# Opening of a mixed mLSTM/S5 decoder step: x turned before the sample state's rows, its squares summed on TensorE, the second weight slab split later

## The chip, the cores and the metric

One Trainium2 chip, one core. The metric is the device time of one execution in microseconds (us), the median of several runs.

## What is computed

One inference step of a two-layer trunk on 576 tokens of 1024 channels: 512 of a fresh prompt and 64 of eight sample sequences (8 tokens each). Layer 0 is an mLSTM matrix memory with 8 heads, layer 1 a grouped complex-diagonal S5 state space; each layer is followed by a squared-ReLU MLP with 4096 hidden channels. What the change touches is the very first norm and the first product:

```
def rms_norm(x, g):
    y = xf * lax.rsqrt(jnp.mean(xf * xf, axis=-1, keepdims=True) + EPS)
    return (y * g)
def mlstm_mixer(x, w_in, ...):
    proj = jnp.einsum('bld,de->ble', x, w_in)      # 1024 -> 3088 columns
    q, k, v, o, gi, gf = jnp.split(proj, ...)
```

All data are float32.

## The kernel before, in words

The activations lie turned: `x[:, k]` holds channels 128k to 128k+127 on the partitions and the 576 tokens along the free axis, so x is 8 tiles (k = 0 to 7; KT = 8) of 128x576. Weights come in slabs of 1024x128 (8 blocks of 128x128), 145 of them. Each slab is used in two parts that together keep float32 precision: ScalarE writes the rounded part `whi` (`split_hi`, L363), VectorE the rest `wlo` (`split_lo`, L368). The activations are split the same way: `prep_hi` (ScalarE, L431) writes `xg_hi`, the rounded x times gain, and `prep_lo` (VectorE, L436) the rest, `xg_lo`. A `product` (L384) is, for each of the 8 tiles, 3 combinations (hi·hi, lo·hi, hi·lo) for 2 halves of 288 tokens: 48 matmuls, shown as 24 pairs. The norm's factor 1/rms is not applied to the input but to the product: `R` holds it for all tokens, and `scale_in` (L1334) multiplies while it takes a slab's result out of PSUM. So product 0 can run before the factor is known, but its result can't leave PSUM.

The order of the work is written out by hand, one program for each engine, tied by semaphores. Each engine executes strictly in its program's order. The opening:

- **SyncE** issues the loads of x (L479, L481), slabs 0 and 1 (L356), the eight rows of the sample state `st_n` (L486, into `nrow`), some small vectors, the S5 matrix `craw`, then slabs 2 and 3. Slab 2 waits for `w_ready` 1 (slab 0 split), slab 3 for `w_ready` 2.
- **TensorE** turns the gains `vrow` (L1847), then the state's rows `nrow` (L1849, waiting for `nrow_in`), then x (loop at L1850 to L1857): for each tile k four 128x128 transposes and one for the 64 sample tokens, into PSUM banks 0/1 or 2/3 in turn. Tile k waits until VectorE has taken out tile k-2. Then product 0, the sum of squares over partitions (`stats`, L394: ones times `acc`, into banks 4 and 5), product 1, product 2, the gate rows (L1873).
- **VectorE** copies the gains and then `nT` (L1318) out of PSUM, then for each tile copies x out (L1324, L1325) and writes `xg_lo` of the tile before; `split_lo` of slab 0 stands after tile 3, that of slab 1 at the end. Then the reciprocal (`inv_rms`, L405), `scale_in` of slab 0, `split_lo` of slab 2, and so on in turn.
- **ScalarE** splits slabs 0 and 1, then for each tile `prep_hi` and the square of x (tile 0 into `acc`, L958; the others alternately into `sqb` and `qkvo[:, 23]`, L962, waiting from k = 3 on until the buffer is free). Then the square root (`rms`, L400).
- **GpSimd** (`square_sums`, L459) adds the squares of tiles 1 to 7 to `acc`, one 128x576 addition a tile.

The same `square_sums` serves the later norms (stages 1 to 3), where it both squares and adds; these stages stay as they are, with their semaphore counts moved.

Of the kernel before, what the change touches and what calls it, by code (L numbers as in the profile page):

```python
# [83 lines left out]
def build(nc, x_prompt, x_sample, st_C, st_n, st_m, st_re, st_im, g_mix, g_ffn, g_fin, w_in, b_i, b_f,  # L84
# [16 lines left out]
    with ctx:  # L101
# [337 lines left out]
        sq0 = (sqb[:], qkvo[:, 23])  # L439

        ACC0 = (0, 8, 16, 23, 31, 36)

        def square_sums(pool, stage):

            n0 = ACC0[stage]
            if stage:
                wait_x(pool, stage, 0)
                nc.gpsimd.tensor_tensor(acc[:], x[:, 0], x[:, 0], ALU.mult).then_inc(acc_done, 1)
            for k in range(1, ACC0[stage + 1] - n0):
                pool.wait_ge(acc_done, n0 + k)  # L450
                if stage:
                    wait_x(pool, stage, k)
                    nc.gpsimd.tensor_tensor(sqb[:], x[:, k], x[:, k], ALU.mult).then_inc(sq_done, 1)
                    pool.wait_ge(sq_done, n0 - KT - (stage - 1) + k)
                    sq = sqb[:]
                else:
                    pool.wait_ge(sq0_done, k)
                    sq = sq0[k % 2]
                nc.gpsimd.tensor_tensor(acc[:], acc[:], sq, ALU.add).then_inc(acc_done, 1)  # L459
# [17 lines left out]
        def _(sp):  # L477
# [26 lines left out]
            def load_u_row(h):  # L504
                if h < 2:
                    sp.wait_ge(ub_out, 16)
                    sp.wait_ge(acc_done, ACC0[1])
                else:
                    sp.wait_ge(exp_done, h - 1)
                sp.dma_start(Ub[h % 2], d_ub[h:h + 1, :].to_broadcast([P, L])).then_inc(ub_in[h % 2], 16)  # L510
# [191 lines left out]
        def _(pool):  # L702
# [9 lines left out]
            square_sums(pool, 0)  # L712
# [214 lines left out]
            pool.wait_ge(sq0_done, 9)  # L927
            nc.gpsimd.tensor_tensor(acc[:], squares[:, 0], squares[:, 1], ALU.add).then_inc(acc_done, 1)  # L928
            for k in range(2, 6):
                pool.wait_ge(sq0_done, 8 + k)  # L930
                pool.wait_ge(acc_done, ACC0[4] + k - 1)
                nc.gpsimd.tensor_tensor(acc[:], acc[:], squares[:, k % 4], ALU.add).then_inc(acc_done, 1)

        @block.scalar
        def _(act):
# [17 lines left out]
            split_hi(act, 1, 0)  # L953
            act.wait_ge(vec_ready, 1)
            for k in range(KT):
                prep_hi(act, k, 0, 0, 0, V_MIX0)
                if k == 0:
                    nc.scalar.activation(acc[:], x[:, 0], ACT.Square).then_inc(acc_done, 1)  # L958
                else:
                    if k >= 3:  # L960
                        act.wait_ge(acc_done, k - 1)
                    nc.scalar.activation(sq0[k % 2], x[:, k], ACT.Square).then_inc(sq0_done, 1)  # L962
# [331 lines left out]
        def _(dve):  # L1294
# [22 lines left out]
            dve.wait_ge(vec_pe, 2)  # L1317
            V.tensor_copy(nT[:], ps[:, 7, 0:32]).then_inc(vec_ready, 1)  # L1318

            for k in range(KT + 1):  # L1320
# [7 lines left out]
                if k in (3, KT):  # L1328
                    split_lo(dve, 0 if k == 3 else 1, 0)
            def scale_in(base, j, t):  # L1330
# [513 lines left out]
        def _(pe):  # L1844
# [3 lines left out]
            pe.wait_ge(nrow_in, 16 * 8)  # L1848
            nc.tensor.transpose(ps[:, 7, 0:32], nrow[:], ident[0:32, 0:32]).then_inc(vec_pe, 1)  # L1849
            pe.wait_ge(x_in, 16 * 5)  # L1850
            for k in range(KT):
# [397 lines left out]
            for a in (acc, tbuf, R):  # L2249
                if a is tbuf:  # L2250
                    pe.wait_ge(sq0_done, 14)
                elif a is R:
                    pe.wait_ge(sq7_done, 2)
# [37 lines left out]
```

## Time and profile before

| | |
|---|---|
| median of 3 runs | 1352.79 us (1350.94 to 1354.02) |
| the profiled execution | 1348.39 us |
| its span in the trace | 1346.6 us |
| TensorE busy | 1295.8 us (96%) |
| VectorE, ScalarE, GpSimd busy | 791.3, 490.5, 355.4 us |
| TensorE's weight loads busy | 1258.2 us (93%) |
| HBM traffic | 121 MB, 90 GB/s over the span |

The span is what the trace covers, from the first instruction to the last; the execution's own time is 1.8 us longer. TensorE is the engine that is nearly always busy, so what counts is where it is idle, where it runs at its lower clock, and how much work it is given. Times within the trace are counted from the span's start.

### The profile page before, as it was taken

What the parts mean: (1) busy time and instruction counts of PE and PEld (TensorE: products, weight loads), DVE (VectorE), ACT (ScalarE), POOL (GpSimd) and SP (SyncE); (2) the same over time, 40 slices, a digit from 0 to 9 for tenths busy, and PEclk for the clock granted to TensorE, in tenths of its full rate; (3) what the DMA queues carried; (4) which work ended last, traced back from release to release, by engine and by line L of the source; (5) the groups of instructions that cost most, each with busy time, mean ns of one, the idle gap of its engine ahead of it and who ended that gap; (6) DMA issues with size and microseconds to landing.
All of it is one profiled execution on the core that took longest, in us unless ns stands there. A gap on an engine that the chain in (4) does not pass through costs nothing.

```text
span 1346.6 us, 24669 instructions
## 1 busy us (share of the span) xinstructions
PE 1295.8 (96%) x9953; PEld 1258.2 (93%) x9953; DVE 791.3 (59%) x1118; ACT 490.5 (36%) x743; POOL 355.4 (26%) x360
## 2 busy tenths in 40 slices
PE   4999999999999999999999899999999999999997
PEld 2999998789999999999999888999999999999997
DVE  5673336867764673342354666343687586686785
ACT  4321136532431331331341124422552442543553
POOL 3001005535899970000027661112000000000001
PEclk9999999999999999999999777999999999999999
DMA  5223332324232232223225995224223323223222
GB/s 150 64 79 85 86 94 73 89 54 104 76 94 79 78 89 82 78 84 87 78 74 150 145 141 125 81 79 124 72 70 94 94 71 116 65 94 96 83 72 71
DMA packets 223039, 121.81 MB, mean 90 GB/s; under 512 B 34752, under 2 KB 218744, under 8 KB 222976
## 3 DMA queue, kind: packets, MB, share of 16 engines
q1 hardware_dynamic: 222144, 120.74, 35.1%
q8 instruction: 42, 0.69, 0.2%
q10 hardware_dynamic: 832, 0.21, 0.1%
q14 instruction: 21, 0.17, 0.1%
HBM read 110.18 MB, written 10.75 MB: 90 GB/s over the span
## 4 chain that ended last, share of the span: by engine, by line
PE 81%; DVE 9%; SPq 3%; DMA 2%; ACT 2%; issue 2%; POOL 1%; ACTq 0%; DVEq 0%; POOLq 0%
PE ps L384 63%; PE ps L2175 12%; DVE wlo L368 1%; PE ps L2131 1%; SPq L628 1%; PE ps L2127 1%; DMA late<-d_taps 1%; SPq L647 1%; DMA Cst<-in_state_mlstm_C 1%; DMA out<-Cst 1%; DVE R L405 1%; DVE x L1660 1%; PE ps L1942 0%; DVE xg_lo L436 0%; DVE hid_lo L1583 0%
## 5 line engine op out<-in xcount | busy, mean ns | idle before, releaser
L384 PE MATMUL ps<-xg_hi,whi 128*128 128x288 f32 x1424 | 304.9, 295 | 3.2 <-DVE wlo L368 1.7
L384 PE MATMUL ps<-xg_hi,wlo 128*128 128x288 f32 x1424 | 304.4, 295 | 0.0
L384 PE MATMUL ps<-xg_lo,whi 128*128 128x288 f32 x1424 | 303.7, 294 | 0.0
L363 ACT ACTIVATE whi<-raw 128x1024 fp32r<-128x1024 f32 x115 | 121.5, 1058 | 353.6 <-PE ps L384 334.1
L384 PEld LDWEIGHTS ps<-xg_hi,whi 128*128 128x128 f32 x1424 | 228.2, 188 | 5.5 <-issue 2.3
L384 PEld LDWEIGHTS ps<-xg_hi,wlo 128*128 128x128 f32 x1424 | 227.7, 188 | 0.0
L384 PEld LDWEIGHTS ps<-xg_lo,whi 128*128 128x128 f32 x1424 | 227.6, 188 | 0.0
L368 DVE TENSOR_TENSOR wlo<-raw,whi 128x1024 fp32r<-128x1024 f32 x115 | 170.3, 1481 | 76.3 <-ACT whi L363 76.2
L384 PE MATMUL ps<-hid_hi,whi 128*128 128x288 f32 x896 | 192.6, 296 | 2.5 <-DVE hid_lo L1805 2.2
L384 PE MATMUL ps<-hid_lo,whi 128*128 128x288 f32 x896 | 192.1, 295 | 0.0
L384 PE MATMUL ps<-hid_hi,wlo 128*128 128x288 f32 x896 | 190.9, 294 | 0.0
L384 PEld LDWEIGHTS ps<-hid_hi,whi 128*128 128x128 f32 x896 | 143.3, 188 | 4.1 <-DVE hid_lo L1805 2.9
L384 PEld LDWEIGHTS ps<-hid_hi,wlo 128*128 128x128 f32 x896 | 143.8, 188 | 0.0
L384 PEld LDWEIGHTS ps<-hid_lo,whi 128*128 128x128 f32 x896 | 143.6, 188 | 0.0
L1561 DVE TENSOR_TENSOR x<-x,ps 128x576 f32 (+1 forms) x40 | 30.2, 754 | 124.7 <-PE ps L384 124.7
L928 POOL TENSOR_TENSOR acc<-hB 128x576 f32<-128x576 f32 x1 | 1.8, 1767 | 350.9 <-ACT hB L1163 350.9
L2175 PE MATMUL ps<-hB_hi,whi 128*128 128x288 f32 x256 | 76.0, 297 | 0.6 <-DVE x L1660 0.6
L1579 DVE TENSOR_TENSOR tbuf<-rbuf,R 128x576 f32<-128x576 f32 x32 | 35.6, 1112 | 68.2 <-ACT rbuf L1067 68.1
L2175 PE MATMUL ps<-hB_hi,wlo 128*128 128x288 f32 x256 | 75.5, 295 | 0.0
L2175 PE MATMUL ps<-hB_lo,whi 128*128 128x288 f32 x256 | 75.4, 294 | 0.0
L1660 DVE TENSOR_TENSOR x<-x,ps 128x288 f32<-128x288 f32 x112 | 50.4, 452 | 32.4 <-PE ps L2175 32.0
L1334 DVE TENSOR_TENSOR qkvo<-ps,R 128x576 f32 (+1 forms) x25 | 18.9, 756 | 77.4 <-PE ps L384 77.3
(401 smaller groups left out, 2066.9 us busy)
## 6 DMA issues: line engine op xcount, KB each, us to landing
raw<-in_ffn_w_up SPq DMA_DIRECT2D x64, 512.0 KB, 4.0
raw<-in_ffn_w_down SPq DMA_DIRECT2D x32, 512.0 KB, 4.2
raw<-in_ffn_w_down SPq DMA_DIRECT2D x16, 1024.0 KB, 5.2
raw<-in_mlstm_w_in SPq DMA_DIRECT2D x25, 512.0 KB, 3.7
raw<-in_s_w_glu SPq DMA_DIRECT2D x16, 512.0 KB, 3.9
raw<-in_mlstm_w_out SPq DMA_DIRECT2D x8, 512.0 KB, 4.2
late<-d_taps SPq DMA_DIRECT2D x32, 128.0 KB, 7.6
d_u<-unat SPq DMA_DIRECT2D x8, 288.0 KB, 2.8
```

The lines of the kernel that those rows point to most:

```text
L363: nc.scalar.activation(whi[:, s], raw[:, s], ACT.Copy).then_inc(whi_done, 1)
L368: nc.vector.tensor_tensor(wlo[:, s], raw[:, s], whi[:, s].bitcast(F32), ALU.subtract).then_inc(w_ready, 1)
L384: last = nc.tensor.matmul(ps[:, 2 * s + c, 0:HN], w[:, s, k, :], a[:, k, c * HN:(c + 1) * HN], start=(k == 0 and n == 0), stop=(k == KT - ...
L405: nc.vector.reciprocal(R[:], R[:]).then_inc(R_ready, 1)
L628: sp.dma_start(U2[i * GC:(i + 1) * GC, g, :], d_u.rearrange("(g c) t b -> t c g b", c=GC)[T - 1 - i, :, g]).then_inc(u2_in[half], 16)
L647: sp.dma_start(taps_pair[j][i * GC:(i + 1) * GC], d_taps[2 * j * P:(2 * j + 2) * P, i * GC:i * GC + P].rearrange("(g c) m -> c g m", c=GC) ...
L1334: V.tensor_tensor(halves(tile(qkvo, t)), slab_ps(s), halves(R[:]), ALU.mult).then_inc(ps_free[s], 1)
L1561: V.tensor_tensor(halves(tile(x, m)), halves(tile(x, m)), slab_ps(s), ALU.add).then_inc(ps_free[s], 1)
L1579: V.tensor_tensor(tbuf[:], rbuf[:], R[:], ALU.mult).then_inc(scaled, 1)
L1660: V.tensor_tensor(xh, xh, ps[:, bank, 0:HN], op).then_inc(x_added, 1)
L2127: nc.tensor.matmul(o[g2], taps_of[k][:, 2 * q + g2, :], U2[:, 8 * k + 2 * q + g2, :], start=True, stop=False)
L2175: last = nc.tensor.matmul(out, w[wi][:, k, :], hi[:, k, t, :], start=(first and k == 0 and n == 0), stop=(k == 3 and n == 2), skip_group_c ...
```

## The change

- TensorE's program turns x right after the gains; the turn of `nrow` stands behind the eight tiles of x, and VectorE's copy `nT` behind its split of slab 1.
- ScalarE writes the squares of all 8 tiles into 8 buffers of their own (`qkvo[:, 16]` to `qkvo[:, 23]`, which slabs fill only later), without waiting for anyone.
- GpSimd has no part in stage 0. `squares_sum(k)` on TensorE multiplies the squares of tile k by ones and accumulates over the tiles in PSUM banks 4 and 5: two float32 matmuls of 288 columns for each tile. Tiles 0 to 5 stand between the transposes of x (behind tile k+2), tiles 6 and 7 inside product 0, before its last two tiles. The old `stats` for stage 0 goes.
- `split_hi` of slab 1 stands behind ScalarE's tile 3, not before tile 0.
- The loads of the first two u rows no longer wait for `acc`.

```diff
-        sq0 = (sqb[:], qkvo[:, 23])
-
-        ACC0 = (0, 8, 16, 23, 31, 36)
+        sq0 = [qkvo[:, 16 + k] for k in range(KT)]
+
+        ACC0 = (0, 0, 8, 15, 23, 28)
...
                 if h < 2:
                     sp.wait_ge(ub_out, 16)
-                    sp.wait_ge(acc_done, ACC0[1])
...
             nc.gpsimd.memset(gw[:, AM, 0:TS + 1:T], 0.0).then_inc(am_ready, 1)
-            square_sums(pool, 0)
...
             split_hi(act, 0, 0)
-            split_hi(act, 1, 0)
             act.wait_ge(vec_ready, 1)
             for k in range(KT):
                 prep_hi(act, k, 0, 0, 0, V_MIX0)
-                if k == 0:
-                    nc.scalar.activation(acc[:], x[:, 0], ACT.Square).then_inc(acc_done, 1)
-                else:
-                    if k >= 3:
-                        act.wait_ge(acc_done, k - 1)
-                    nc.scalar.activation(sq0[k % 2], x[:, k], ACT.Square).then_inc(sq0_done, 1)
+                nc.scalar.activation(sq0[k], x[:, k], ACT.Square).then_inc(sq0_done, 1)
+                if k == 3:
+                    split_hi(act, 1, 0)
             rms(act, 0)
...
             V.tensor_copy(vec[:].rearrange("p v k -> p (v k)"), ps[:, 4, 0:56]).then_inc(vec_ready, 1)
-            dve.wait_ge(vec_pe, 2)
-            V.tensor_copy(nT[:], ps[:, 7, 0:32]).then_inc(vec_ready, 1)
-
             for k in range(KT + 1):
...
                     split_lo(dve, 0 if k == 3 else 1, 0)
+            dve.wait_ge(vec_pe, 2)
+            V.tensor_copy(nT[:], ps[:, 7, 0:32]).then_inc(vec_ready, 1)
...
-            pe.wait_ge(nrow_in, 16 * 8)
-            nc.tensor.transpose(ps[:, 7, 0:32], nrow[:], ident[0:32, 0:32]).then_inc(vec_pe, 1)
             pe.wait_ge(x_in, 16 * 5)
+
+            def squares_sum(k):
+                if k == 0:
+                    pe.wait_ge(vec_ready, 1)
+                    pe.wait_ge(const_done, 2)
+                pe.wait_ge(sq0_done, k + 1)
+                for c in range(2):
+                    last = nc.tensor.matmul(ps[:, 4 + c, 0:HN], ones[:], sq0[k][:, c * HN:(c + 1) * HN],
+                                            start=(k == 0), stop=(k == KT - 1))
+                if k == KT - 1:
+                    last.then_inc(stat_done, 1)
+
             for k in range(KT):
...
                 nc.tensor.transpose(ps[:, r + 1, 0:TS], xtok[0:TS, 0, k * P:(k + 1) * P],
                                     ident[0:TS, 0:TS]).then_inc(xt_done, 1)
+                if k >= 2:
+                    squares_sum(k - 2)
+            pe.wait_ge(nrow_in, 16 * 8)
+            nc.tensor.transpose(ps[:, 7, 0:32], nrow[:], ident[0:32, 0:32]).then_inc(vec_pe, 1)
             pe.wait_ge(x_ready, KT - 1)
-            pe.wait_ge(const_done, 2)
             xg, hid = (xg_hi, xg_lo), (hid_hi, hid_lo)
-            product(pe, 0, 0, xg, (xg_ready, 0))
-            pe.wait_ge(vec_ready, 1)
-            stats(pe, 0)
+            product(pe, 0, 0, xg, (xg_ready, 0), range(KT - 2))
+            for k in range(KT - 2, KT):
+                squares_sum(k)
+            product(pe, 0, 0, xg, (xg_ready, 0), range(KT - 2, KT))
             pe.wait_ge(x_ready, KT)
             product(pe, 1, 0, xg)
```

The rest of the diff moves the semaphore counts of the later stages.

TensorE's program at the start, before (`xtok` is x as loaded, `vrow` the gains, `nrow` the state's rows):

```order
L1847 MATMUL ps<-ident,vrow 128x56 [waits vec_in,const_done]
L1849 MATMUL ps<-ident,nrow 128x32 [waits nrow_in]
L1856 MATMUL ps<-ident,xtok 128x128 [waits x_in]
L1856 MATMUL ps<-ident,xtok 128x128 x3
L1857 MATMUL ps<-ident,xtok 128x64
```

and now (`ones` with `qkvo` is a square's sum; the tiles that follow repeat the last five rows):

```order
L1834 MATMUL ps<-ident,vrow 128x56 [waits vec_in,const_done]
L1853 MATMUL ps<-ident,xtok 128x128 [waits x_in]
L1853 MATMUL ps<-ident,xtok 128x128 x3
L1854 MATMUL ps<-ident,xtok 128x64
L1853 MATMUL ps<-ident,xtok 128x128 x4
L1854 MATMUL ps<-ident,xtok 128x64
L1853 MATMUL ps<-ident,xtok 128x128 [waits x_ready]
L1853 MATMUL ps<-ident,xtok 128x128 x3
L1854 MATMUL ps<-ident,xtok 128x64
L1843 MATMUL ps<-qkvo,ones 128x288 [waits sq0_done,const_done,vec_ready]
L1843 MATMUL ps<-qkvo,ones 128x288
```

The turn of x has moved ahead of that of `nrow`, and from the third tile on a sum of squares, which waits for ScalarE, stands between the tiles.

TensorE's program around the end of product 0, one piece of the difference:

```order
 L384 MATMUL ps<-xg_hi,wlo 128x288 x2
+L1843 MATMUL ps<-qkvo,ones 128x288 [waits sq0_done]
+L1843 MATMUL ps<-qkvo,ones 128x288
+L1843 MATMUL ps<-qkvo,ones 128x288 [waits sq0_done]
+L1843 MATMUL ps<-qkvo,ones 128x288
 L384 MATMUL ps<-xg_hi,whi 128x288 [waits xg_ready]
 L384 MATMUL ps<-xg_hi,whi 128x288
...
 L384 MATMUL ps<-xg_hi,wlo 128x288 x2
-L394 MATMUL ps<-acc,ones 128x288 [waits acc_done,vec_ready]
-L394 MATMUL ps<-acc,ones 128x288
 L384 MATMUL ps<-xg_hi,whi 128x288 [waits w_ready,x_ready]
```

The last two sums stand two tiles ahead of the end of product 0, where the single one stood behind it.

## Rows read from the trace of the kernel before

**Rows 1.** The page: busy time by engine.
```profile
PE 1295.8 (96%) x9953; PEld 1258.2 (93%) x9953; DVE 791.3 (59%) x1118; ACT 490.5 (36%) x743; POOL 355.4 (26%) x360
```

**Rows 2.** Chain of waits, 0 to 90 us: start, duration, what.
```profile
12.93 2.86 DMA nrow<-in_state_mlstm_n
...
39.17 0.98 PE ps L394 x4
```

**Rows 3.** Last load of x: issue, and its time to landing.
```profile
L481 SPq DMA_DIRECT2D xtok<-in_x_prompt x1: 436/436/436, 3.0 to 3.0; - x1
...
DMA to landing us min/median/max: 8.0/8.0/8.0
```

**Rows 4.** Timeline of TensorE, 16 to 35 us: start, duration, instruction, idle before.
```profile
16.08 1.11 PE L1856 MATMUL ps<-ident,xtok 128*128 128x128 f32 x4
...
17.42 1.11 PE L1856 MATMUL ps<-ident,xtok 128*128 128x128 f32 x4
...
26.88 1.12 PE L1856 MATMUL ps<-ident,xtok 128*128 128x128 f32 x4 [2.69 <-DVE x L1325]
...
33.25 0.68 PE L384 MATMUL ps<-xg_lo,whi 128*128 128x288 f32 x2
33.73 0.68 PE L384 MATMUL ps<-xg_hi,wlo 128*128 128x288 f32 x2
```

**Rows 5.** Timeline of TensorE, end of product 1 and start of product 2.
```profile
45.54 0.43 PE L384 MATMUL ps<-xg_hi,whi 128*128 128x288 f32 x2
45.80 0.42 PE L384 MATMUL ps<-xg_lo,whi 128*128 128x288 f32 x2
46.07 0.43 PE L384 MATMUL ps<-xg_hi,wlo 128*128 128x288 f32 x2
46.69 0.54 PE L384 MATMUL ps<-xg_hi,whi 128*128 128x288 f32 x2 [0.20 <-DVE wlo L368]
```

**Rows 6.** Timeline of ScalarE, 12 to 20 us.
```profile
12.88 1.06 ACT L363 ACTIVATE whi<-raw 128x1024 fp32r<-128x1024 f32 x1 [2.51 <-DMA raw<-in_mlstm_w_in]
...
18.44 0.78 ACT L431 ACTIVATE xg_hi<-x,vec 128x576 fp32r<-128x576 f32 x1 [3.05 <-DVE x L1325]
...
19.72 0.78 ACT L431 ACTIVATE xg_hi<-x,vec 128x576 fp32r<-128x576 f32 x1
```

**Rows 7.** Timeline of VectorE, 18 to 46 us.
```profile
20.33 0.69 DVE L1324 COPY x<-ps 128x512 f32<-128x512 f32 x1
...
21.78 0.69 DVE L1324 COPY x<-ps 128x512 f32<-128x512 f32 x1
...
23.68 2.41 DVE L368 TENSOR_TENSOR wlo<-raw,whi 128x1024 fp32r<-128x1024 f32 x1
...
40.96 3.75 DVE L405 RECIPROCAL R<-R 128x576 f32<-128x576 f32 x1 [3.25 <-ACT R L400]
44.74 0.76 DVE L1334 TENSOR_TENSOR qkvo<-ps,R 128x576 f32<-128x576 f32 x1
45.42 1.22 DVE L368 TENSOR_TENSOR wlo<-raw,whi 128x1024 fp32r<-128x1024 f32 x1
```

**Rows 8.** Eight transposes of the S5 matrix, later, on TensorE.
```profile
83.06 1.09 PE L1883 MATMUL ps<-ident,craw 128*128 128x128 f32 x8
```

**Rows 9.** Timeline of TensorE in the S5 layer, 775 to 841 us.
```profile
775.75 2.24 PE L2112 MATMUL ps<-U,GT 128*64 128x72 f32 x32
...
836.10 0.85 PE L384 MATMUL ps<-hid_hi,whi 128*128 128x288 f32 x2
...
840.00 0.42 PE L384 MATMUL ps<-hid_hi,wlo 128*128 128x288 f32 x2
```

**Rows 10.** Table by stretch: busy us of PE, PEld, DVE, ACT, POOL; granted clock; DMA.
```profile
770.00:775.00 5.00, 5.00 (x31) 4.34 (x30) 3.77 (x7) 0.00 (x0) 3.75 (x4) 0.50 1.39 108
775.00:780.00 5.00, 5.00 (x60) 4.65 (x58) 1.93 (x5) 2.00 (x5) 0.62 (x1) 0.66 1.29 114
...
835.00:840.00 5.00, 5.00 (x26) 4.83 (x26) 0.00 (x0) 1.88 (x4) 0.00 (x0) 0.52 0.57 128
```

More of the change, by code:

```diff
@@ L437, in prep_lo @@
                                            ALU.mult, ALU.subtract).then_inc(xg_ready, 1)
-        sq0 = (sqb[:], qkvo[:, 23])
-        ACC0 = (0, 8, 16, 23, 31, 36)
+        sq0 = [qkvo[:, 16 + k] for k in range(KT)]
+        ACC0 = (0, 0, 8, 15, 23, 28)
         def square_sums(pool, stage):
             n0 = ACC0[stage]
-            if stage:
-                wait_x(pool, stage, 0)
-                nc.gpsimd.tensor_tensor(acc[:], x[:, 0], x[:, 0], ALU.mult).then_inc(acc_done, 1)
+            wait_x(pool, stage, 0)
+            nc.gpsimd.tensor_tensor(acc[:], x[:, 0], x[:, 0], ALU.mult).then_inc(acc_done, 1)
             for k in range(1, ACC0[stage + 1] - n0):
                 pool.wait_ge(acc_done, n0 + k)
[L451 to L455, printed above, removed]
-                else:
-                    pool.wait_ge(sq0_done, k)
-                    sq = sq0[k % 2]
-                nc.gpsimd.tensor_tensor(acc[:], acc[:], sq, ALU.add).then_inc(acc_done, 1)
+                wait_x(pool, stage, k)
+                nc.gpsimd.tensor_tensor(sqb[:], x[:, k], x[:, k], ALU.mult).then_inc(sq_done, 1)
+                pool.wait_ge(sq_done, n0 - (stage - 1) + k)
+                nc.gpsimd.tensor_tensor(acc[:], acc[:], sqb[:], ALU.add).then_inc(acc_done, 1)
         def last_squares(dve, stage):
@@ L926, in _ @@
             squares = hB[:].rearrange("p (s h) c -> p s (h c)", h=2)
-            pool.wait_ge(sq0_done, 9)
+            pool.wait_ge(sq0_done, KT + 2)
             nc.gpsimd.tensor_tensor(acc[:], squares[:, 0], squares[:, 1], ALU.add).then_inc(acc_done, 1)
             for k in range(2, 6):
-                pool.wait_ge(sq0_done, 8 + k)
+                pool.wait_ge(sq0_done, KT + 1 + k)
                 pool.wait_ge(acc_done, ACC0[4] + k - 1)
@@ L956, in _ @@
                 prep_hi(act, k, 0, 0, 0, V_MIX0)
-                if k == 0:
-                    nc.scalar.activation(acc[:], x[:, 0], ACT.Square).then_inc(acc_done, 1)
-                else:
-                    if k >= 3:
-                        act.wait_ge(acc_done, k - 1)
-                    nc.scalar.activation(sq0[k % 2], x[:, k], ACT.Square).then_inc(sq0_done, 1)
+                nc.scalar.activation(sq0[k], x[:, k], ACT.Square).then_inc(sq0_done, 1)
+                if k == 3:
+                    split_hi(act, 1, 0)
             rms(act, 0)
@@ L2250, in _ @@
                 if a is tbuf:
-                    pe.wait_ge(sq0_done, 14)
+                    pe.wait_ge(sq0_done, KT + 7)
                 elif a is R:
```

## The prediction, made before the changed kernel had run

> **What bounds the kernel now.** I read the page first: TensorE is busy 96% of the span [rows 1], so the kernel gets faster only where TensorE starts earlier, waits less, has less to do or runs at a better clock. The change touches the first 40 us alone, so I then read the chain of waits and the timelines there. The reader is to see one long detour. The last part of x was issued at 3.0 and needed 8.0 us: x is there at 11.0 [rows 3]. But TensorE's next instruction is the turn of the state's rows, whose last load was issued at 12.9 and took 2.9 us [rows 2]; it ran at 15.8, and x's first transposes at 16.1 [rows 4]. Five microseconds go by with x on the chip. After that TensorE turns x, a tile every 1.34 us (16.08 to 17.42 [rows 4]), stands still for 2.7 us at 24.2 to 26.9 for VectorE (the split of slab 0 took 2.41 us [rows 7], twice the 1.22 that the same instruction on slab 2 takes once GpSimd no longer adds squares), reaches product 0 at 31.2, and is solid from there: the sum of squares runs for 0.98 us from 39.0 (39.17 in the chain, which starts it at its second matmul's record [rows 2]), product 1 follows, and product 2 begins at 46.69, some 0.35 us late, since the chain square root, reciprocal (3.75 us), scale-out of slab 0, split of slab 2 has only just ended [rows 5, 7]. The mark by which I measure is that start of product 2 at 46.69: from there on both kernels have the same program, and each engine is released by TensorE's products.
>
> **TensorE's two speeds.** A pair of 288-column matmuls starts every 0.48 us in the first three microseconds of product 0 (33.25 to 33.73 [rows 4]) and every 0.265 us later (45.54 to 46.07 in two steps [rows 5]). The same 0.48 stands in the S5 layer where the granted clock reads 0.50, and it becomes 0.26 where that goes back to 1.00 [rows 9, 10]. So the first stretch ran at the 1.2 GHz level, though no granted clock is recorded for it, and it rose to 2.4 GHz at 34.2. What the engine did before a rise: 3.0 us of product 0; 3.7 us of products (836.1 to 839.8 [rows 9]); 2.6 us of closely packed 72-column matmuls (775.75 to about 778.4, by the 0.66 of that row [rows 9, 10]). The 8 us of transposes from 16.1 on brought no rise.
>
> **The change, part by part.**
>
> *The turn of nrow moves behind x.* The gains were taken out at 10.5 already, so x starts when it is there, at 11.05 instead of 16.08: 5.0 us earlier. The nrow turn costs 0.3 us in its new place, where its load is long there. VectorE's copy of 0.2 us stands behind its split of slab 1 and nobody needs it before the gate rows.
>
> *ScalarE.* It splits slab 0 at 12.88, when the slab lands, until 13.94 [rows 6]. This is not moved and is now on the path: tile 0 of x is out of PSUM by 13.3. Rounding and squaring one tile take 1.28 us (18.44 to 19.72 [rows 6]), so the first squares are ready at about 15.3. The split of slab 1, 1.06 us, moves behind tile 3. ScalarE's eight tiles and that split take at most 8 x 1.46 + 1.06 = 12.7 us from 13.9 on (1.46 is VectorE's pace), so 27, plus a table load of 1.3: no sum has to wait for it (the last one is due above 31, below).
>
> *GpSimd's seven additions go.* They were not on TensorE's path by themselves, but VectorE was slow beside them. Without them I take VectorE's undisturbed pace, 1.45 us for a tile (20.33 to 21.78 [rows 7]) and 1.14 to 1.22 for a split. From the first copy at 12.5 that is 12.5 + 8 x 1.45 + 2 x 1.2 = 26.5, with its waits for TensorE below some 28 to 29; product 0 needs its tiles one by one from 27 on. The 2.7 us stall goes; what is late next is TensorE itself.
>
> *The squares' sum on TensorE.* One pair of float32 matmuls of 288 columns costs 0.98 us at the high clock [rows 2]; eight instead of one add 6.9 us. At the low clock the trace has none: between 0.98 x 0.48/0.265 = 1.78 and 0.98 x 2 = 1.96; I take 1.94, near the upper end, as the pair is four records of pure streaming. So from 15.3, when the first sum is released, TensorE never runs dry. All at the high clock it would have to do: 5 tiles of transposes at 0.68 (8 transposes take 1.09 [rows 8], so five 0.68) = 3.4; 8 sums x 0.98 = 7.84; nrow 0.2; product 0, 24 pairs x 0.265 = 6.36. Together 17.8, so product 1 at 33.1. Of the time c spent at the low clock half is lost. The squares are dense float32 work, so I expect the rise among them, but they are broken up by transposes: between 2.6 us (the quickest rise above) and 7 us after 15.3. I take c = 4.5, near the rises seen (3.0, 3.7) plus an allowance for the transposes between. That costs 2.25: product 1 at 35.4, its end 6.35 later at 41.7.
>
> *The square root's chain.* The last sum ends two product tiles (1.6 us) before product 1, at 33.8; square root 0.74, reciprocal 3.75, scale-out 0.76, split 1.22 [rows 7] end at 40.4, 1.3 us before 41.7. The 0.35 us wait of product 2 goes too.
>
> *Sum.* Product 2 starts at 41.7 instead of 46.7: **5.0 us saved**; with c from 2.6 to 7, 5.9 to 3.7. The later stages are released by products and shift as a whole. The loads of u rows waited on `acc` in name only, and the renumbered semaphores cost nothing. Against the profiled execution that gives 1348.4 - 5.0 = 1343.4. That execution was 4.4 us quicker than the median of the runs, 1352.8, which is what the forecast is for: **1347.8 us**. The runs lie within 3 us of each other, and about 0.2% (2.7 us) is what can be told from no change.
>
> **A rule against it.** Eight microseconds of transposes, a tile every 1.34 us, brought no rise of the clock [rows 4]. The Trainium skill (TensorE: Matmul & The Clock Gate, Part 4: PE-mode transpose) says the full clock doesn't engage for transposes, since they don't count as busy in the same way; the trace agrees, as far as those 8 us go. If that keeps the mixture low as well, the sum is that of the first rival.
>
> **The rivals.**
>
> *A, the low clock lasts through the squares (slower).* If transposes between the sums keep TensorE at 1.2 GHz, it has from 15.3 to do 6 x 1.94 + 5 x 1.34 + 0.3 = 18.6 us before product 0, which then starts at 33.9, later than the 31.2 of before. It is followed by 6.36 + 2 x 0.98 and half of another 3.0: product 1 at 43.8, product 2 at 50.2, 3.5 us later than now: 1356.3. For it: 8 us of transposes gave no rise, and they would be 40% of the mixture's time. Against it: 2.6 us of dense short matmuls behind a thinner mixture sufficed in the S5 layer. The point at which it decides: with c above about 14 us nothing is gained. Chance 0.10.
>
> *B, a late rise or a wait that takes over (no change).* With c of 10 to 14 us, or an engine that I take as covered (ScalarE's tiles behind the slab split at 13.9, VectorE, a later landing of x or slab 0) costing 3 us, the gain is 0 to 2.5: about 1351.5. For it: ScalarE and TensorE now hand each tile to one another through VectorE, with margins of a microsecond. Chance 0.18.
>
> *C, the gain arrives and is bigger.* If the rise comes within 2.6 us and transposes at the high clock are cheaper than 0.68 a tile, 6 to 6.5 us: 1346.5. It is the low side of the forecast, not a case apart.
>
> **How the numbers follow.** Forecast with C 0.72, B 0.18, A 0.10. The forecast's own range is 1345.3 (6.5 saved, and one for the runs' spread) to 1350. To hold 8 in 10 the range takes in most of B: 1345.0 to 1352.4; A and the last of each side stay out. Faster by over 0.2%: 0.72; within: 0.18; slower: 0.10.
>
> **What would show it.** Right: the first transposes of x at about 11.1, the first sum at 15.3, no gap on TensorE of more than a few tenths until product 2; a pair of sums falling from 1.9 to 0.98 us between 18 and 22; VectorE's split of slab 0 at 1.2 us; product 0 from about 27, product 2 at 41.7; later stages of the same lengths. Wrong: sums still at 1.9 us when product 0 starts (A), or TensorE idle between tiles (B), or a stage behind 50 us that has grown by what was saved.

## The result, and the profile after

The changed kernel took 1342.16 us (median of 7 runs, 1337.76 to 1344.28), the kernel before 1350.00 us (median of 7, 1345.13 to 1354.02; three of the seven are the runs that the prediction knew, the other four, 1345.13 to 1350.00, have a median of 1346.7). The ratio is 0.9948, 95% interval 0.9923 to 0.9973: 7.0 us faster, 3.6 to 10.4. (Here and below the ratio with its interval is an estimate over the runs and not the quotient of the two medians, which lie 7.8 us apart.) The predicted saving of 5.0 us lies in that interval; the predicted time of 1347.8 us is 5.6 us too high, and the measured time is outside the range. The profiled execution of the changed kernel took 1343.77 us, that of before 1348.39: 4.6 us.

The page of the changed kernel: busy time, the chain by line.

```profile
PE 1300.7 (97%) x9981; PEld 1262.1 (94%) x9981; DVE 786.0 (59%) x1118; ACT 490.2 (37%) x743; POOL 343.4 (26%) x353
...
PE ps L384 64%; PE ps L2176 12%; PE ps L2132 1%; PE ps L2128 1%; DVE wlo L368 1%; PE ps L1843 1%; DMA Cst<-in_state_mlstm_C 1%; DMA xtok<-in_x_prompt 1%; DMA late<-d_taps 1%; DMA out<-Cst 1%; DVE x L1647 1%; PE ps L1853 0%; PE ps L2113 0%; ACT qkvo L1008 0%; PE ps L2070 0%
```

Beside [rows 1]: TensorE has 28 matmul records and 4.9 us of busy time more, GpSimd 12 us less, and the span is 4.8 us shorter. An engine that is given more work finishes earlier; the time came out of its idle stretches (50.8 us before, 41.1 now). The load of x (`xtok`) has entered the chain in the place of `nrow`'s [rows 2].

TensorE's timeline of the changed kernel, 10 to 43 us (start, duration, instruction, idle before it and its releaser):

```profile
10.93 1.12 PE L1853 MATMUL ps<-ident,xtok 128*128 128x128 f32 x4 [1.55 <-DMA xtok<-in_x_prompt]
...
12.28 1.11 PE L1853 MATMUL ps<-ident,xtok 128*128 128x128 f32 x4
...
15.16 2.26 PE L1843 MATMUL ps<-qkvo,ones 128*128 128x288 f32 x4
17.21 1.06 PE L1853 MATMUL ps<-ident,xtok 128*128 128x128 f32 x4
...
18.50 1.68 PE L1843 MATMUL ps<-qkvo,ones 128*128 128x288 f32 x4
20.01 0.60 PE L1853 MATMUL ps<-ident,xtok 128*128 128x128 f32 x4
...
20.74 1.24 PE L1843 MATMUL ps<-qkvo,ones 128*128 128x288 f32 x4
21.82 0.60 PE L1853 MATMUL ps<-ident,xtok 128*128 128x128 f32 x4
...
27.33 0.24 PE L1859 MATMUL ps<-ident,nrow 32*128 32x32 f32 x1
27.50 0.53 PE L384 MATMUL ps<-xg_hi,whi 128*128 128x288 f32 x2
...
32.37 2.10 PE L1843 MATMUL ps<-qkvo,ones 128*128 128x288 f32 x8
34.09 0.65 PE L384 MATMUL ps<-xg_hi,whi 128*128 128x288 f32 x2
...
42.23 0.43 PE L384 MATMUL ps<-xg_hi,whi 128*128 128x288 f32 x2
```

Read the starts. x is turned at 10.93 (16.08 before [rows 4]), a tile every 1.35 us, the low level of the clock. The first sum takes from 15.16 to 17.21, 2.05 us; the second from 18.50 to 20.01, 1.51 us; the third from 20.74 to 21.82, 1.08 us: the clock rose to its 2.4 GHz level at about 19.4, within the second. From there on a tile and its sum take 1.81 us. No idle time stands beside any row after the first. Product 0 starts at 27.50; 42.23 is product 2's start, for there are 24 pairs before it from 35.89 on, and no wait stands there (46.69, with a wait, before [rows 5]).

VectorE's and ScalarE's timelines of the changed kernel, the rows that answer to [rows 6, 7]:

```profile
18.60 0.69 DVE L1309 COPY x<-ps 128x512 f32<-128x512 f32 x1 [1.85 <-PE ps L1854]
...
20.07 1.22 DVE L368 TENSOR_TENSOR wlo<-raw,whi 128x1024 fp32r<-128x1024 f32 x1
...
35.28 3.75 DVE L405 RECIPROCAL R<-R 128x576 f32<-128x576 f32 x1 [5.29 <-ACT R L400]
39.07 0.76 DVE L1321 TENSOR_TENSOR qkvo<-ps,R 128x576 f32<-128x576 f32 x1
39.74 1.22 DVE L368 TENSOR_TENSOR wlo<-raw,whi 128x1024 fp32r<-128x1024 f32 x1
```

```profile
12.72 1.06 ACT L363 ACTIVATE whi<-raw 128x1024 fp32r<-128x1024 f32 x1 [2.22 <-DMA raw<-in_mlstm_w_in]
13.68 0.76 ACT L431 ACTIVATE xg_hi<-x,vec 128x576 fp32r<-128x576 f32 x1
14.35 0.67 ACT L948 ACTIVATE qkvo<-x 128x576 f32<-128x576 f32 x1
...
34.51 0.74 ACT L400 ACTIVATE R<-ps,eps 128x576 f32<-128x576 f32 x1 [4.72 <-PE ps L1843]
```

The split of slab 0 takes VectorE 1.22 us, not 2.41 [rows 7]. VectorE waits for TensorE now (1.85 us), where TensorE waited 2.69 us for VectorE [rows 4]. ScalarE's first square ends at about 15.0 and releases the first sum. The chain of square root, reciprocal, scale-out and split ends at 41.0, 1.3 us before product 2 asks for its slab.

### The profile page after: what moved, and what is told of

It reads as the page before. It is cut to its first block, busy times and chain, and to the rows that moved or that the text cites. A ratio compares the mean times of both kernels' runs of the same rounds, so it can differ in the third digit from the quotient of the medians.

```text
span 1341.8 us, 24708 instructions
## 1 busy us (share of the span) xinstructions
PE 1300.7 (97%) x9981; PEld 1262.1 (94%) x9981; DVE 786.0 (59%) x1118; ACT 490.2 (37%) x743; POOL 343.4 (26%) x353
## 4 chain that ended last, share of the span: by engine, by line
PE 84%; DVE 7%; ACT 3%; DMA 2%; issue 2%; SPq 1%; POOL 1%; ACTq 0%; DVEq 0%; POOLq 0%
PE ps L384 64%; PE ps L2176 12%; PE ps L2132 1%; PE ps L2128 1%; DVE wlo L368 1%; PE ps L1843 1%; DMA Cst<-in_state_mlstm_C 1%; DMA xtok<-in_x_prompt 1%; DMA late<-d_taps 1%; DMA out<-Cst 1%; DVE x L1647 1%; PE ps L1853 0%; PE ps L2113 0%; ACT qkvo L1008 0%; PE ps L2070 0%
```

## The experiments

Times of all runs are medians of the runs beside their own runs of the kernel before. Three more readings are used below. *The gate rows' start*: where TensorE begins L1873 (53.23 in the profile before, 48.67 in that of the changed kernel, so 4.56 us earlier); it closes the part that the change touches. *The marks*: the start of the same matmul, counted back from the program's last, in two profiles. *At equal clock*: each timed run records the mean granted clock of its span; over all single runs of all kernels one line was fitted, with a level for each kernel (two for the change, one for each set of its runs). It says 1.1 us for 0.001 of mean clock, with 1.8 us of scatter about it. No granted clock is recorded before the first rise, so the opening's low stretch isn't in that mean, and the difference of two levels is what the opening is worth, as long as no recorded fall lies in it, no wait comes up later, and the change doesn't itself lower the mean clock. Where it does that, this reading leaves out a loss that the kernel has. The +/- is a 95% interval.

**The kernel before, again, twice.** Is the opening stable, and what varies?

> The kernel before itself, for a second profile of it. Theory S: its opening is the same to within a microsecond wherever it is run (the turn of nrow at 15 to 16, the gate rows at 52.2 to 53.3), while the rest of the span moves by several us with the stretches at the 1.2 GHz level behind 750 us; the first three runs, at 1352.8, were at the slow end of that spread. Rival: the opening itself varies by 3 us or more, which would make the comparison of single profiles worthless.

> The same once more, a third profile of the kernel before: the gate rows again at 52.2 to 53.3 by theory S, and a span that differs from the other two by what TensorE's low-clock stretches differ, half of their length.

They took 1346.82 and 1344.54 us, against 1348.39. The gate rows started at 52.38 and 52.97, within 0.9 us of the first profile and inside the expected 52.2 to 53.3. Of the third profile's 3.8 us 0.3 lie in the opening, of the second's 1.5 us 0.85. A difference under a microsecond between the openings of two single profiles is therefore no finding. The third's mean clock is 0.984 against 0.980, for which the line gives 4.4 us.

**The changed kernel again,** unedited.

> The changed kernel once more, unedited, beside the kernel before on one chip. Theory S (the opening is all there is): what the change saves is what the opening shows, product 2 starting 4.5 us earlier; the rest of the difference between the two medians (7.8 us) is run-to-run spread from how long TensorE is at the 1.2 GHz level in later stages. Then the ratio comes out nearer 0.9965 (4.7 us), product 2 starts at 42 to 43, and among single runs a higher mean granted clock goes with a shorter time, about 3.4 us for 0.0025. Theory L (something later got shorter too): the ratio stays at 0.994 to 0.995 (7 to 8 us), and at the same mean clock the changed kernel is still 7 us ahead; a stage behind 50 us is shorter in the trace.

1340.47 us (12 runs, 1338.12 to 1345.35). The kernel before took 1347.54 us in 35 runs, from 1337.71 to 1353.10. Ratio 0.9959 (0.9936 to 0.9982): 5.5 us, nearer the 4.7 expected of the opening alone than the 7 to 8 of something later; the interval holds both. TensorE's timeline of this run:

```profile
9.84 1.11 PE L1853 MATMUL ps<-ident,xtok 128*128 128x128 f32 x4 [0.35 <-DMA xtok<-in_x_prompt]
...
14.08 2.26 PE L1843 MATMUL ps<-qkvo,ones 128*128 128x288 f32 x4 [0.15 <-ACT qkvo L948]
...
17.24 1.24 PE L1843 MATMUL ps<-qkvo,ones 128*128 128x288 f32 x4
...
46.97 1.38 PE L1874 MATMUL ps<-qkvo,ident 128*8 128x288 f32 x5
```

x landed 1.1 us earlier than in the first profile, and so did slab 0 (ScalarE split it at 11.64). The gate rows start at 46.97, 6.3 us before those of the kernel before and 1.7 before those of the first profile of the change. Of the 1.7 us 1.1 are the landings. The other 0.6 are the clock, which rose at 16.9, 2.8 us after the first sum began, and not 4.3 us after it: the second sum, from 17.24, already has the fast price of 1.07. So these landings are now on the path at their full length, where `nrow` hid them. In both profiles slab 0's is the later one in what it releases: ScalarE takes tile 0 the moment its split of slab 0 ends, half a microsecond after VectorE has copied tile 0. At equal clock the two sets of runs give 5.1 +/- 1.4 and 5.9 +/- 1.2 us.

**The order alone:** the kernel before with only the turn of `nrow` and its copy `nT` moved.

```diff
-            pe.wait_ge(nrow_in, 16 * 8)
-            nc.tensor.transpose(ps[:, 7, 0:32], nrow[:], ident[0:32, 0:32]).then_inc(vec_pe, 1)
             pe.wait_ge(x_in, 16 * 5)
             for k in range(KT):
...
+            pe.wait_ge(nrow_in, 16 * 8)
+            nc.tensor.transpose(ps[:, 7, 0:32], nrow[:], ident[0:32, 0:32]).then_inc(vec_pe, 1)
```

> The kernel before with only the turn of nrow (TensorE) and the copy nT (VectorE) moved behind x; the squares stay with GpSimd. Theory S: ScalarE now starts tile 0 behind its two slab splits, at 15.4 instead of 18.4, and everything else keeps the old pace (VectorE slow beside GpSimd), so product 2 at 43.7, 3.0 us saved. Rival (order alone is the whole gain): product 2 at 42.2, 4.5 us saved, the squares' move being worth nothing.

1344.68 us, ratio 0.9985 (0.9962 to 1.0008). Its timeline of TensorE:

```profile
10.78 1.11 PE L1853 MATMUL ps<-ident,xtok 128*128 128x128 f32 x4 [0.50 <-DMA xtok<-in_x_prompt]
...
23.16 1.12 PE L1853 MATMUL ps<-ident,xtok 128*128 128x128 f32 x4 [2.82 <-DVE x L1322]
...
27.43 0.85 PE L384 MATMUL ps<-xg_hi,whi 128*128 128x288 f32 x2 [0.75 <-DVE x L1322]
...
43.58 0.53 PE L384 MATMUL ps<-xg_hi,whi 128*128 128x288 f32 x2 [0.20 <-DVE wlo L368]
```

Product 2 at 43.58, gate rows 3.1 us earlier, 3.1 +/- 1.2 at equal clock. x starts 5.3 us earlier and 2.2 of it go. The first 1.6 go at the start, where VectorE waits for ScalarE's first tile:

```profile
15.87 0.82 DVE L436 SCALAR_TENSOR_TENSOR xg_lo<-x,vec,xg_hi 128x576 fp32r<-128x576 f32 x1 [1.48 <-ACT xg_hi L431]
```

In the profile before this row stands at 19.60, so VectorE's tiles, and with them product 0, come 3.7 us earlier and not 5.3: ScalarE splits slabs 0 and 1 first and reaches tile 0 only at 15.07. The other 0.6 are a later rise, 4.5 us into product 0 where it was 3.1. GpSimd's additions slow VectorE as they did before (the split of slab 0 takes 2.42 us, TensorE's stall 2.82), so they cost this kernel nothing new; they are what it has not yet got rid of.

**The squares' sum alone:** the change with the turn of `nrow` and `nT` back in their old places.

```diff
+            pe.wait_ge(nrow_in, 16 * 8)
+            nc.tensor.transpose(ps[:, 7, 0:32], nrow[:], ident[0:32, 0:32]).then_inc(vec_pe, 1)
             pe.wait_ge(x_in, 16 * 5)
...
-            pe.wait_ge(nrow_in, 16 * 8)
-            nc.tensor.transpose(ps[:, 7, 0:32], nrow[:], ident[0:32, 0:32]).then_inc(vec_pe, 1)
             pe.wait_ge(x_ready, KT - 1)
```

> The changed kernel with the turn of nrow and the copy nT put back ahead of x. Theory S: x's first transposes at 16.1 again, first sum at 19.8; from there TensorE has the same 17.8 us at the high clock plus about 2 for the low one as with the whole change, so product 2 at 46 to 46.5: 0.2 to 0.7 us saved, alone no change that can be told. Rival (the squares' move is what pays): product 2 at 44 or earlier.

1344.74 us, ratio 0.9990 (0.9967 to 1.0013); x turned at 15.24, first sum at 19.27, gate rows 0.35 us earlier, 0.6 +/- 1.2 at equal clock. Alone the sums fill the stall that they remove and save nothing that can be told. The two give 3.1 and 0.35 us, the whole change 4.6 and 6.3. What is missing need not be an effect of the two together, for there is a third part, the split of slab 1 behind tile 3. The order alone is without it, and by its rows would have been spared most of the 1.6 us of waiting; here it brings nothing, since ScalarE waits 3.53 us for tile 0 in any case. With the 1.5 us that it is worth below, the parts add up to 5.0. No run has the order and the split without the squares, so this is argued and not shown.

**All sums inside product 0:** the price of adding them where nothing stands still.

```diff
-                if k >= 2:
-                    squares_sum(k - 2)
...
-            for k in range(KT - 2, KT):
+            for k in range(KT):
                 squares_sum(k)
```

> The changed kernel with all eight sums of squares inside product 0 (ahead of its last two tiles), none between the transposes. Theory I (the sums are cheap because they stand where TensorE would be idle beside VectorE's copies): transposes at the 1.2 GHz level throughout, product 0 already at about 23.5, some 4 us earlier than with the change, but then 7.8 us of sums in front of the square root: product 1 at 39.4, product 2 at about 45.8, nearly 4 us later than with the change. Rival (where the sums stand doesn't matter, only that GpSimd is out of VectorE's way): product 2 at 42 to 43.

```profile
23.18 0.85 PE L384 MATMUL ps<-xg_hi,whi 128*128 128x288 f32 x2
...
30.20 7.92 PE L1843 MATMUL ps<-qkvo,ones 128*128 128x288 f32 x32
37.74 0.65 PE L384 MATMUL ps<-xg_hi,whi 128*128 128x288 f32 x2
```

Eight sums in 7.54 us (30.20 to 37.74), 0.94 each at the high clock. The gate rows start at 52.32, 3.65 us later than in the change; one run took 1345.14 us. The sums pay where they stand: between the transposes, on a TensorE that would wait or run at the low clock.

**The split of slab 1 back in front:** `split_hi(act, 1, 0)` before tile 0, not behind tile 3.

> The changed kernel with ScalarE's split of slab 1 back ahead of tile 0. Theory P (ScalarE's first tile is on the path of the first sum): it starts behind the second split, at 15.2 instead of 13.7, the first sum at 16.7, and everything up to product 2 moves by 1.5 us, to 43.6. Rival (the split is hidden in either place): product 2 at 42.1 to 42.4.

```profile
16.19 2.26 PE L1842 MATMUL ps<-qkvo,ones 128*128 128x288 f32 x4 [1.65 <-ACT qkvo L949]
```

The first sum waits 1.65 us for ScalarE, although slab 0 had landed 0.5 us earlier than in the first profile: this part of the change is worth about 1.5 us, the 1.06 us of the split and 0.46 in which ScalarE waits for slab 1 to land. The gate rows start at 49.11, only 0.44 us later than in the first profile of the change, because the earlier landing gave back 0.5 and the clock rose 2.8 us after the first sum began, as in the repeat, and not 4.3. That puts product 2 at about 42.7, between the 43.6 of the theory and the 42.1 to 42.4 of its rival; the wait settles it, the end of the opening alone would not have. Yet this run took 1336.94 us, less than any run of the change. Its opening doesn't explain that; what comes later does, as the table below shows.

**Does an earlier rise bring more?** 26 float32 matmuls whose result nobody uses stand ahead of the turn of the gains.

```diff
-            pe.wait_ge(const_done, 1)
+            pe.wait_ge(const_done, 2)
+            for i in range(26):
+                nc.tensor.matmul(ps[:, 6, 0:P], ones[:], ones[:], start=True, stop=True)
```

> The changed kernel with 26 extra float32 matmuls (ones by ones, 128 columns, into a PSUM bank not yet used) on TensorE while it waits for the gains, from about 2 to 9.5 us. Their result is not used. Theory S: the time lost to the low clock among the sums (15.2 to 19.4, half of it, 2.1 us) comes back; sums cost 0.98 us from the first on, product 2 at about 40.1, 6.6 us before the kernel before. Rival W (the 1.5 us of idleness before x lands, or the transposes, let the clock fall again): sums start at 1.9 us as before, product 2 at 42.2. Rival D (VectorE and ScalarE can't follow): product 2 at 41.5, with gaps on TensorE between the tiles.

```profile
10.96 0.66 PE L1855 MATMUL ps<-ident,xtok 128*128 128x128 f32 x4
...
11.75 0.66 PE L1855 MATMUL ps<-ident,xtok 128*128 128x128 f32 x4
...
15.07 2.26 PE L1845 MATMUL ps<-qkvo,ones 128*128 128x288 f32 x4 [1.48 <-ACT qkvo L948]
17.12 1.06 PE L1855 MATMUL ps<-ident,xtok 128*128 128x128 f32 x4
```

The transposes run at 0.79 us a tile, but the first sum is due only when ScalarE has squared tile 0, so TensorE stands still for 1.48 us, and the clock has fallen when it goes on (the granted clock is recorded as risen from 8.0 to 14.8): 2.05 us for that sum again. That is rival W. 1343.63 us, ratio 0.9987 (0.9964 to 1.0009), gate rows 5.14 us earlier, no better than the change.

**Keeping it up:** 18 such matmuls ahead of the gains' turn and 3 behind each of tiles 0 to 2.

> The changed kernel with 18 extra float32 matmuls before the gains' turn and 3 more behind each of the first three tiles of x, so that TensorE has dense work up to the first sum. In the kernel with one block of extra matmuls the clock rose at 8.0 and fell again at 14.8, after 3 us of transposes and 1.5 us of idleness. Theory F (what let it fall was that thin stretch): no fall, every sum at 0.98 us; first sum at 15.1 as ScalarE sets it, product 2 at 40.1. Rival (the clock falls on its own once transposes begin): first sums at 1.9 us again, product 2 at 42 or later.

```profile
14.34 0.94 PE L1836 MATMUL ps<-ones 128*128 128x128 f32 x6
15.11 1.14 PE L1849 MATMUL ps<-qkvo,ones 128*128 128x288 f32 x4
16.08 0.60 PE L1859 MATMUL ps<-ident,xtok 128*128 128x128 f32 x4
```

No fall: the first sum takes 0.97 us, product 0 starts at 25.38, the gate rows 6.7 us earlier, which is product 2 at 40.1 as expected. One run, 1342.56 us.

**The same with tile 0 ahead of slab 0's split on ScalarE,** to release the first sum sooner.

```diff
-            split_hi(act, 0, 0)
...
-                if k == 3:
-                    split_hi(act, 1, 0)
+                if k in (1, 3):
+                    split_hi(act, k // 2, 0)
```

> As the kernel with fillers, and ScalarE's split of slab 0 stands behind its tile 1 instead of ahead of tile 0. ScalarE then starts with tile 0 when VectorE has copied it, at about 12.7 instead of 13.7. Theory F: first sum at 14.2, product 2 at about 39.2, and against the kernel before 6.5 to 7.5 us at equal mean clock, 1 to 2 us better than the change alone. Rival (the slab's split is then late for VectorE, which splits slab 0 behind tile 3, and TensorE waits there): product 2 at 40 to 41.

A miss. The gains came late (TensorE turned them at 10.25, after 2.38 us of idle time), the clock fell at 12.4, and the extra matmuls, now at the low clock, held up x: first sum at 17.12, gate rows 4.7 us earlier. 1342.92 us, ratio 0.9964 (0.9949 to 0.9979).

**The sums in the rounded form:** the squares are written rounded (type fp32r), so the sum loses their last bits, and one sum is two matmul records, where the full one is four.

```diff
-        sq0 = [qkvo[:, 16 + k] for k in range(KT)]
+        sq0 = [sqr[:, 16 + k] for k in range(KT)]
...
-                    last = nc.tensor.matmul(ps[:, 4 + c, 0:HN], ones[:], sq0[k][:, c * HN:(c + 1) * HN],
+                    last = nc.tensor.matmul(ps[:, 4 + c, 0:HN], sqr[:, 15, 0:P], sq0[k][:, c * HN:(c + 1) * HN],
```

> The changed kernel with the sums of squares in the rounded float32 form that the products use: ScalarE writes the squares and a block of ones into a tile of that type, so a sum costs one pass for each 288 columns in place of four. The squares lose their last bits by it. Theory D (dense sums bring the clock up): a sum takes 0.48 us at the 1.2 GHz level, the mixture with the transposes (1.34 us a tile) is thin, and the clock stays down until some 3 us into product 0; product 0 at about 25, product 1 at 33.6, product 2 at about 40.2 and the gate rows at 46.6 to 47.7, 1 to 2 us earlier than with the change although the sums themselves shrank by 5.7 us. Rival (the clock rises among the transposes all the same, at 18 to 20): product 0 at 23.5 or before, the gate rows at 45 or before.

```profile
15.15 0.82 PE L1847 MATMUL ps<-sqr 128*128 128x288 f32 x2 [0.33 <-ACT sqr L952]
15.77 1.05 PE L1857 MATMUL ps<-ident,xtok 128*128 128x128 f32 x4
...
29.78 0.59 PE L386 MATMUL ps<-xg_hi,wlo 128*128 128x288 f32 x2
30.20 0.42 PE L386 MATMUL ps<-xg_hi,whi 128*128 128x288 f32 x2
```

A sum takes 0.62 us, and the clock stays low until 30.1, 4.3 us into product 0, as expected. The gate rows start 5.75 us earlier. 1340.96 us (11 runs, 1331.62 to 1348.67), ratio 0.9950 (0.9925 to 0.9976); the change's 0.9959 cannot be told from it.

**Both:** rounded sums, 22 extra matmuls ahead, one behind the gains, two behind each tile.

> Rounded sums, and 22 extra float32 matmuls before the gains' turn, 1 behind it and 2 behind each tile of x. Theory D: the clock is up from about 7 us on and stays up, so a tile of x with its sum and its fillers costs TensorE 1.4 us, no more than VectorE's 1.45; product 0 then starts when VectorE is ready, at about 23.5, sums and product at the high clock, product 1 at 30.4, the gate rows at about 43.3, 10 us earlier than in the kernel before; ratio about 0.992 to 0.993. Rival (what is saved at the opening comes back later, in a wait on slabs or on VectorE's scaling of slab 0): the gate rows at 45 to 46. Rival W (the clock falls between gains and x): 2 us less.

```profile
15.11 0.51 PE L1854 MATMUL ps<-sqr 128*128 128x288 f32 x2 [0.36 <-ACT sqr L952]
...
23.64 0.53 PE L386 MATMUL ps<-xg_hi,whi 128*128 128x288 f32 x2
```

The opening did what was expected: gate rows 9.8 us earlier (43.40). The time did not: 1342.45 us, ratio 0.9972 (0.9959 to 0.9986), a gain of 3.8 us, where a ratio of 0.992 to 0.993 was expected. The mean clock of its 12 runs was 0.9782, that of the 22 runs of the kernel before beside it 0.9819. The difference of 0.0037 is five times its standard error of 0.0007, so it isn't spread: this kernel runs at a lower mean clock, and the line prices that at 4 us. At equal clock it is 8.4 +/- 1.2 us, which leaves this loss out; what the kernel gains is the 3.8.

**Where the rest goes.** The start of the same matmul, less its start in the profile before (us; the columns are that profile's times):

| profile | gate rows, 53 | 204 | 300 | 750 | 819 | end, 1339 |
|---|---|---|---|---|---|---|
| before, again | -0.85 | -0.86 | -0.27 | -0.34 | -1.24 | -1.52 |
| before, third | -0.26 | -0.27 | -1.25 | -1.25 | -0.31 | -3.80 |
| changed | -4.56 | -4.55 | -4.18 | -4.21 | -5.42 | -5.34 |
| changed, again | -6.26 | -4.74 | -0.32 | -0.37 | -5.26 | -7.41 |
| order alone | -3.11 | -1.98 | -1.97 | -1.97 | -0.15 | -4.23 |
| squares alone | -0.35 | -0.35 | -2.09 | -2.16 | -3.46 | -3.78 |
| sums in product 0 | -0.91 | +0.24 | -0.65 | -0.68 | -3.09 | -3.27 |
| split of slab 1 in front | -4.12 | -2.58 | -4.32 | -4.36 | -9.97 | -12.05 |
| extra matmuls ahead | -5.14 | -3.62 | -2.20 | -2.27 | -0.19 | -4.18 |
| extra, kept up | -6.68 | -6.69 | -4.85 | -4.89 | -6.41 | -6.32 |
| the same, tile 0 first | -4.66 | -4.66 | -2.91 | -2.96 | -2.32 | -5.28 |
| rounded sums | -5.75 | -4.52 | -2.76 | -2.78 | -2.26 | -6.17 |
| rounded, extra matmuls | -9.83 | -9.82 | -8.10 | -8.03 | -6.72 | -7.00 |

Between 300 and 750 every kernel keeps its lead to 0.1 us. The differences arise before 204 (in some), in the mLSTM's work on its heads (205 to 280) and in the S5 layer (757 to 840), whose programs the change leaves as they were. There the table by stretch (columns as in [rows 10]) shows one reason, the clock; first the changed kernel, then the same kernel in the repeat:

```profile
265.00:275.00 10.00, 8.81 (x67) 7.62 (x68) 8.33 (x33) 3.25 (x16) 6.16 (x13) 1.00 0.24 66
...
780.00:785.00 5.00, 5.00 (x44) 4.48 (x45) 0.22 (x1) 1.16 (x4) 2.77 (x3) 0.50 1.20 124
785.00:790.00 5.00, 5.00 (x50) 4.56 (x47) 3.90 (x8) 1.12 (x2) 2.14 (x2) 0.76 1.23 132
```

```profile
265.00:275.00 10.00, 7.90 (x41) 6.36 (x40) 5.57 (x17) 3.05 (x14) 5.57 (x12) 0.72 0.22 58
...
780.00:785.00 5.00, 5.00 (x46) 4.42 (x44) 4.83 (x11) 1.02 (x1) 4.00 (x4) 0.85 1.23 122
785.00:790.00 5.00, 5.00 (x74) 4.55 (x73) 3.35 (x8) 2.29 (x5) 4.84 (x5) 1.00 1.20 129
```

The same kernel runs 265 to 275 at a granted clock of 1.00 in one execution and 0.72 in the next, and between the marks at 204 and 300 the second loses 4.4 us of its lead, the first 0.4. In the S5 layer the second is back at 1.00 by 785, the first only after it; from 750 to 819 the second gains 4.9 us, the first 1.2. The run with the split in front had fewer such stretches (mean clock 0.985), and they are most of what brings it to 1336.94 us.

The clock is not the only reason. In the repeat a wait stands ahead of the fall at 269; first the changed kernel, then the repeat:

```profile
265.90 0.19 POOL L746 COPY Cst<-nT 128x4 f32<-128x4 f32 x1 [2.55 <-DMA Cst<-in_state_mlstm_C]
...
268.67 0.66 PE L1958 MATMUL ps<-ident,Htok 128*128 128x128 f32 x4 [0.57 <-DVE Htok L1518]
```

```profile
266.31 0.19 POOL L746 COPY Cst<-nT 128x4 f32<-128x4 f32 x1 [4.34 <-DMA Cst<-in_state_mlstm_C]
...
268.81 0.66 PE L1958 MATMUL ps<-ident,Htok 128*128 128x128 f32 x4 [2.10 <-DVE Htok L1518]
```

GpSimd waits longer for a load of the matrix state, VectorE for GpSimd, and TensorE for VectorE: 1.5 us of the lead are gone before the clock falls. The wait of about 2 us stands in the profiles of the repeat, of all three kernels with extra matmuls and full sums, and of both with rounded sums, and in none of the other eight, the three of the kernel before among them. In four of these six the clock falls right behind it; in the other two the wait alone takes 1.4 us, with rounded sums and extra matmuls 1.4 of the 9.8. A second one is TensorE's wait for the S5 taps (`late` from `d_taps`): 3.0 us in the profile before, 1.5 and 1.8 in the two of the change, 5.7 in the third of the kernel before, 6.5 with rounded sums and extra matmuls.

So falls of the clock come with every version (the 35 runs of the kernel before spread over 15.4 us with them), but not all of what is lost later is independent of the change. A fall near 80 us, worth 1.1 to 1.5 us, stands in six of the ten profiles in which x is turned first and in none of the four in which it isn't; with so few profiles that may be chance. And a lower mean clock is clear of spread with rounded sums and extra matmuls (above) and with extra matmuls ahead (0.9787 in 12 runs against 0.9811 in 35, three times the standard error), not in the change itself (0.9815 against 0.9811). Why is open. With extra matmuls ahead a part is that the record of the clock begins earlier and counts the fall in the opening (0.0013 of the mean in the profiled execution); with rounded sums and extra matmuls the opening has no fall.

## Why the prediction was right in its steps and wrong in its number

- *x at 11.05:* 10.93. Hit. In the repeat 9.84; the path now carries the landings of x and slab 0, which moved by more than a microsecond and which the prediction took as fixed.
- *The first sum at 15.3, released by ScalarE behind slab 0:* 15.16. Hit.
- *The low clock lasts c = 4.5 us from there, half lost:* the rise came at 19.4, so c = 4.3. Hit, and in part luck: the same program gave c = 2.8 in the repeat, and in the other profiles without extra matmuls the rise came 2.9 to 5.2 us after the first full sum or, where there is none, after the first product. That alone moves the sum by up to 0.8 us. The price of a sum at the low clock was 1.94; it measured 2.05, nearly double the 1.08 between transposes at the high clock.
- *The 17.8 us of work:* from 15.16, 17.8 and 2.15 (half of 4.3) give product 1 at 35.1; it started at 35.89 (24 pairs of 0.265 us ahead of 42.23). Mis-sized by 0.8 us: at the high clock a tile and its sum took 1.81 us, not 0.68 + 0.98 = 1.66, which is 0.6 over four of them, and the first pairs behind other work in product 0 took 0.38 and 0.48 us, not 0.265, 0.3 more; the two sums inside product 0 took 1.72 together, 0.2 less than 2 x 0.98.
- *VectorE at its undisturbed pace once GpSimd's additions are gone:* splits of 1.22 instead of 2.41, no stall. Hit. With the additions and the new order the 2.42 and a 2.82 us stall are there (the order alone).
- *The square root's chain with 1.3 us to spare:* 41.0 against 42.2. Hit.
- *Product 2 at 41.7, 5.0 us saved:* 42.23, 4.5 saved; the gate rows 4.6; in the repeat 6.3; at equal clock 5.1 and 5.9; by the ratios 7.0 and 5.5. The size is right. Against the profiled execution, 1343.4 was forecast and 1343.8 measured; that it agrees to 0.4 us is partly luck, since three profiled executions of the kernel before span 3.9 us.
- *The rivals:* A (the low clock lasts through the squares) fell with the rise at 19.4; the rounded sums show that it was real, since there the same mixture with thinner sums gave no rise in 10 us. B's condition, an engine taken as covered that is not, is what the experiment with slab 1's split in front makes: 1.65 us of waiting, not the 3 that B needs.

**The step that failed** is the last: "That execution was 4.4 us quicker than the median of the runs, 1352.8, which is what the forecast is for: 1347.8 us. The runs lie within 3 us of each other". Three runs were taken for the kernel's spread. In 35 runs the kernel before has a median of 1347.5 and a range of 15.4 us, so the three lay at the upper end, the base was some 5 us too high, and the one us allowed for spread in the range was too little. The result itself says the same: the four runs of the kernel before that the prediction hadn't seen have a median of 1346.7, and 1346.7 less the forecast 5.0 is 1341.7, against 1342.16 measured. The step added 4.4 us to a sum that needed nothing added: the profiled execution, 1348.4, was the better sample of the kernel. The shown [rows 9, 10] already held the main reason, stretches in the S5 layer at a granted clock of 0.50 to 0.66; what the prediction did not ask is whether they fall the same way in each execution. They don't, as the marks show. One reading of these rows was too narrow as well: ahead of the rise at 778.4 stand not only 2.6 us of 72-column matmuls, for TensorE had worked without a gap since 767.3, still at the low level.

On the rule of the Trainium skill (TensorE: Matmul & The Clock Gate, Part 4: PE-mode transpose), that the full clock doesn't engage for transposes: that 8 us of transposes alone gave no rise agrees. The fall in the run with extra matmuls, behind three tiles of them, doesn't decide it, since idle time stood there too. But their own duration is not tied to the low clock: four took 1.11 us at the low level and 0.60 at the high one.

The Trainium skill (SBUF — State Buffer, SBUF: two separate sides) says of VectorE and GpSimd that the shared port pair is "an **exclusive lock**, not a bandwidth split". The slab's split took 2.41 us beside GpSimd's additions and 1.22 without them; that agrees in direction, while which of the additions blocked it was not measured apart.

## What to carry to other kernels

Work added to the busiest engine can save time if it stands where that engine waits or runs at its low clock, and dense work there also brings the rise forward; the same sums placed inside a solid product cost their full 0.94 us each. When a late load is taken off the path, the next arrival stands behind it (here slab 0, x and ScalarE's first square), so its spread and the order of the engine that serves it count from then on. Where the granted clock falls in stretches that differ between executions, forecast the difference of two kernels, read the single runs together with their mean clock, and take no base from three runs. But don't take the figure at equal clock for the gain: compare the mean clocks of the two kernels first, since a change can lower its own.

## What the runs showed of the hardware that was not expected

- The clock of one kernel falls in other places from execution to execution: 1.1 us per 0.001 of mean granted clock over all single runs, and with it 1337.7 to 1353.1 us for the kernel before.
- The rise comes at different times in one program: 4.3 us after the first sum in one execution of the changed kernel, 2.8 in another, which moved everything behind it by 0.6 us.
- A clock that is up is lost easily: after three tiles of transposes (2.6 us) and 1.2 us of idle time it fell; with three float32 128-column matmuls behind each tile it stayed up; with 2.38 us of idle time ahead of the gains' turn and 0.49 behind it, it fell at 12.4, although the first three stood there.
- An opening 9.8 us shorter gave 3.8 us in the ratio, and 8.4 at equal clock. Of the rest 1.4 us are one longer wait in the profile, and some 4 are a mean clock lower by 0.0037, five standard errors, whose cause is open.
